# A transformer layer on one core: output tiles finished in pairs, weight splits ahead of finishing steps, and a later threshold search

## The reference, cut to what matters

```python
mix = einsum('bte,ed->btd', concatenate([att_out, hg_out]), w_out)   # 2048 x 1024 x 1024
x   = x + rms_norm(mix, norm_post_mix)
h2  = rms_norm(x, norm_pre_ffn)
ff  = silu(h2 @ w_gate) * (h2 @ w_up)                                 # 1024 -> 2816
ff  = ff @ w_down                                                     # 2816 -> 1024
x   = x + rms_norm(ff, norm_post_ffn)
```

## Time and profile before

| | us |
|---|---|
| median of the three runs | 3438.05 |
| lowest and highest of the three | 3437.49, 3439.71 |
| the profiled execution, its own time | 3442.69 |
| the span of its profile | 3440.9 |
| TensorE matmul busy | 3241.5 (94%) |
| VectorE busy | 2249.4 (65%) |
| ScalarE busy | 1500.5 (44%) |
| mean granted TensorE clock | 0.972 |

### The profile page before, as it was taken

The page is one execution under the profiler, slowest core; times in us unless marked ns, Lnnn a source line. Parts: engine busy times, 40 slices in busy tenths (PEclk is TensorE's granted clock), DMA queues, the critical chain, the costliest instruction groups (busy, mean ns, idle before and its releaser), DMA issues. The chain is left out here.

```text
span 3440.9 us, 46671 instructions
## 1 busy us (share of the span) xinstructions
PE 3241.5 (94%) x18176; PEld 2861.3 (83%) x18176; DVE 2249.4 (65%) x3721; ACT 1500.5 (44%) x2477; POOL 241.9 (7%) x400
## 2 busy tenths in 40 slices
PE   8999999999788799999979999997999999979998
PEld 8999999999666688888768888876988888868886
DVE  3466776888565676666777777778776765464445
ACT  3444545455354444343445444445454444333222
POOL 0000010000110100010110001011000000010000
PEclk9999999999899899999989999998999999989999
DMA  5434343434221322222422222134121111242233
GB/s 181 157 118 151 115 144 117 138 119 129 102 77 56 120 73 85 74 85 74 159 97 67 73 74 76 65 112 145 58 68 62 65 59 62 92 171 98 92 101 107
DMA packets 147501, 345.75 MB, mean 100 GB/s; under 512 B 15056, under 2 KB 35920, under 8 KB 145232
## 3 DMA queue, kind: packets, MB, share of 16 engines
q1 hardware_dynamic: 144976, 338.55, 29.4%
q10 hardware_dynamic: 2304, 4.20, 0.3%
HBM read 283.38 MB, written 59.31 MB: 100 GB/s over the span
## 5 line engine op out<-in xcount | busy, mean ns | idle before, releaser
L2018 PE MATMUL PJ_d<-h_hi,wd_hi 128*128 128x512 f32 (+1 forms) x1472 | 575.3, 391 | 13.8 <-DVE h_lo L1783 12.1
L2020 PE MATMUL PJ_d<-h_hi,wd_lo 128*128 128x512 f32 (+1 forms) x1472 | 563.5, 383 | 0.0
L2019 PE MATMUL PJ_d<-h_lo,wd_hi 128*128 128x512 f32 (+1 forms) x1472 | 562.4, 382 | 0.0
L1534 ACT ACTIVATE wd_hi<-wd_raw 128x512 fp32r<-128x512 f32 x568 | 345.7, 628 | 253.6 <-DMA wd_raw<-in_w_gu 160.8
L713 PE MATMUL PJ<-w_hi,h_hi 128*128 128x342 f32 (+1 forms) x1280 | 416.3, 325 | 5.9 <-DVE w_lo L539 5.9
L1778 DVE TENSOR_TENSOR wd_lo<-wd_raw,wd_hi 128x512 fp32r<-128x512 f32 x568 | 381.9, 690 | 47.0 <-ACT wd_hi L1534 44.2
L1529 ACT ACTIVATE pT<-SA 128x512 f32<-128x512 f32 (+3 forms) x320 | 156.5, 531 | 584.8 <-PE SA L1964 584.7
L714 PE MATMUL PJ<-w_lo,h_hi 128*128 128x342 f32 (+1 forms) x1280 | 409.4, 320 | 0.0
L715 PE MATMUL PJ<-w_hi,h_lo 128*128 128x342 f32 (+1 forms) x1280 | 409.3, 320 | 0.0
L1763 DVE CUSTOM_DVE_ANT_0 prob<-SA,bias 128x1024 f32<-128x1024 f32 (+7 forms) x192 | 170.1, 912 | 323.9 <-PE SA L1938 323.3
L2018 PEld LDWEIGHTS PJ_d<-h_hi,wd_hi 128*128 128x128 f32 x1472 | 279.5, 190 | 63.8 <-issue 11.8
(11 more groups left out here) (202 smaller groups left out, 5776.5 us busy)
## 6 DMA issues: line engine op xcount, KB each, us to landing
wd_raw<-in_w_gu SPq DMA_DIRECT2D x352, 256.0 KB, 3.0
wd_raw<-in_w_down SPq DMA_DIRECT2D x176, 256.0 KB, 2.6
w_raw<-in_w_in SPq DMA_DIRECT2D x40, 684.0 KB, 4.6
w_raw<-in_w_in SPq DMA_DIRECT2D x40, 676.0 KB, 4.5
row_h<-proj_d SPq DMA_DIRECT2D x16, 1024.0 KB, 6.7
proj_d<-stage SPq DMA_DIRECT2D x40, 342.0 KB, 4.5
proj_d<-stage SPq DMA_DIRECT2D x40, 338.0 KB, 5.0
x_d<-acc SPq DMA_DIRECT2D x24, 512.0 KB, 2.6
```

The source lines that it names most:

```text
L1534: s_.activation(w_hi[:, u % RING, :], w_raw[:, u % RING, :], ACT.Copy).then_inc(w_hi_ready, 1)
L2018: t.matmul(to[:, tok], w_hi[:, r, w], h_hi[:, c, tok], start=(c == 0 and part != 1), stop=False)
L2019: t.matmul(to[:, tok], w_hi[:, r, w], h_lo[:, c, tok], start=False, stop=False)
L2020: last = t.matmul(to[:, tok], w_lo[:, r, w], h_hi[:, c, tok], start=False, stop=(c == KD - 1 and part != 0))
```

## The change

The out items of a superblock run in pairs of tiles: both halves of tiles 0 and 1, then both of tiles 2 and 3. The turns of tiles 2 and 3 stand between the out items. Before, all four turns of s = 0 stood ahead of its outs, those of tiles 2 and 3 of s = 1 and 2 and of tile 2 of s = 3 among the last down items, and that of tile 3 of s = 3 behind the third out item. All turns and outs of s = 0 lie beside block 4, before and after. The transposes of the normalised tiles 0 and 1 come right after the last out item (gaps 0 and 1), and those of tiles 2 and 3 between the first halves of up 0. In VectorE's step the weight splits stand in front of `finish`. In blocks 4, 8 and 12 the threshold search begins at head 3 instead of head 0 and ends at the same place. SyncE's loads follow: the gains of s = 0 are loaded before its first turn, and for later superblocks norm_post_mix waits for all four finished tiles at the fourth out item; x of tiles 2 and 3 of s = 0 is loaded after turns 0 and 1, before after turn 3.

```diff
+    SEARCH = {(0, "A"): (0,), (0, "B"): (1,), (1, "A"): (2,), (2, "A"): (3,), (2, "B"): (4,), (3, "A"): (5,), (4, "A"): (6,),
+              (4, "B"): (7,), (5, "A"): (8,), (6, "A"): (9,), (6, "B"): (10,), (7, "A"): (11,)}
+    LATE_SEARCH = {(3, "A"): (0,), (3, "B"): (1,), (4, "A"): (2,), (4, "B"): (3, 4), (5, "A"): (5,), (5, "B"): (6, 7),
+                   (6, "A"): (8, 9), (6, "B"): (10,), (7, "A"): (11,)}
+    def search(b, h, name):
+        return (LATE_SEARCH if b and b % TS == 0 else SEARCH).get((h, name), ())
...
-    items += [("turn", 0, i) for i in range(TS)]
+    OUTS = [(n, i) for pair_of in range(0, TS, 2) for n in range(2) for i in (pair_of, pair_of + 1)]
     for s in range(NS):
-        outs = [("out", s, kg, n, i) for kg in range(1) for n in range(2) for i in range(TS)]
-        items += outs if s + 1 < NS else outs[:3] + [("turn", s, 3)] + outs[3:]
+        outs = [("out", s, 0, n, i) for n, i in OUTS]
+        if s == 0:
+            FIRST = len(items)
+            items += [("turn", 0, 0), ("turn", 0, 1)] + outs[:4] + [("turn", 0, 2), outs[4], ("turn", 0, 3)] + outs[5:]
+        elif s < LAST:
+            items += [outs[0], ("turn", s, 2), outs[1], ("turn", s, 3)] + outs[2:]
+        else:
+            items += [outs[0], ("turn", s, 2)] + outs[1:5] + [("turn", s, 3)] + outs[5:]
         first = [("up", s, 0, m, half, part) for part in range(2) for m in range(2) for half in range(2)]
-        items += [("gap", s, 0), ("gap", s, 1), ("gap", s, 2), ("gap", s, 3), first[0], ("gap", s, 4), first[1], first[2],
-                  ("gap", s, 5)] + first[3:]
+        items += [("gap", s, 0), ("gap", s, 1)] + first[:3] + [("gap", s, 2), first[3], ("gap", s, 3)] + first[4:]
...
-                if x == ("part", EARLY[-1], 1, 1, 2):
+                if x == ("part", EARLY[-1], 1, 1, 0):
                     load_mix(0, 0)
                     load_mix(0, 1)
+                    load_gain("norm_post_mix", g_mix_in)
+                    load_gain_ffn()
...
+                if x[0] == "out" and s and x[3:] in OUTS[:TS]:
+                    i = OUTS.index(x[3:])
+                    if i == TS - 1:
+                        sp.wait_ge(out_ready, TS * s)
                         load_gain("norm_post_mix", g_mix_in)
                         load_gain_ffn()
-                if x[0] == "out" and s and x[2:4] == (0, 0):
-                    i = x[4]
                     store_out(s - 1, i)
...
                 if last_out(n - 3):
                     add_mix(item_at(n - 3)[1], item_at(n - 3)[4])
+                for u in splits_at.get(n - 1, []):
+                    split_unit(u)
                 if last_down(n - 4):
                     finish(item_at(n - 4)[1], item_at(n - 4)[4])
-                for u in splits_at.get(n - 1, []):
-                    split_unit(u)
...
                     fill(("A", b, h))
-                    g = h // 2
-                    topk_part(b + 1, 3 * g if h % 2 == 0 else 3 * g + 2)
+                    for k in search(b, h, "A"):
+                        topk_part(b + 1, k)
                     fill(("B", b, h))
-                    if h % 2 == 0:
-                        topk_part(b + 1, 3 * g + 1)
+                    for k in search(b, h, "B"):
+                        topk_part(b + 1, k)
```

More of the change, by code:

```diff
@@ L861, in mixer_phase @@
                     items.append(("down", s, g, n, i))
-                    if g == NG - 1 and n == 0 and s + 1 < NS and i < (2 if s + 2 < NS else 1):
-                        items.append(("turn", s + 1, 2 + i))
     at = {x: n for n, x in enumerate(items)}
@@ L964, in mixer_phase @@
             window = window[PARTS_FROM:]
-            last = PARTS - 1
+            last = FIRST - 1
         mine = [x[0] for x in items[done:last + 1]]
@@ L1104, in enter_items @@
                     enter(key, "h")
-                if x[0] == "gap" and x[2] >= 2:
-                    h_order["hT", x[1], x[2] - 2] = len(h_order)
-                    enter(("hT", x[1], x[2] - 2), "h")
+                if x[0] == "gap":
+                    h_order["hT", x[1], x[2]] = len(h_order)
+                    enter(("hT", x[1], x[2]), "h")
         def enter_slot(key):
@@ L1589, in step @@
                     turned_high(("mT", x[1], x[2]), x[2], 0, KD // 2)
-                if x[0] == "gap" and x[2] >= 2:
-                    if x[2] == 2:
+                if x[0] == "gap":
+                    if x[2] == 0:
                         wait_summed(act, x[1], TS - 1)
-                    turned_high(("hT", x[1], x[2] - 2), x[2] - 2, 0, KD)
+                    turned_high(("hT", x[1], x[2]), x[2], 0, KD)
                 for u in splits_at.get(n, []):
@@ L1623, in _ @@
                         fill(("C", b, h))
-                    if h % 2 == 0:
-                        count(b + 1, 3 * (h // 2) + 1)
+                    for k in search(b, h, "B"):
+                        count(b + 1, k)
                 if b + 1 < NB:
@@ L1868, in step @@
                     norm_x1(item_at(n - 5)[1], item_at(n - 5)[4])
[L1869 to L1870 removed]
+                if x[0] == "gap":
+                    turned_low(("hT", x[1], x[2]), x[2], 0, KD)
                 if last_out(n - 3):
                     add_mix(item_at(n - 3)[1], item_at(n - 3)[4])
+                for u in splits_at.get(n - 1, []):
+                    split_unit(u)
                 if last_down(n - 4):
                     finish(item_at(n - 4)[1], item_at(n - 4)[4])
[L1875 to L1876 removed]
             def fill(key):
@@ L1996, in item @@
                     turn(("mT", s, x[2]), tile[:, mix_home(x[2]), :], KD // 2)
-                if x[0] == "gap" and x[2] >= 2:
-                    pe.wait_ge(xn_ready, TS * s + x[2] - 1)
-                    turn(("hT", s, x[2] - 2), tile[:, X_HOME[x[2] - 2], :], KD)
+                if x[0] == "gap":
+                    pe.wait_ge(xn_ready, TS * s + x[2] + 1)
+                    turn(("hT", s, x[2]), tile[:, X_HOME[x[2]], :], KD)
                 if x not in done_count:
```

16 lines of the change are left out of this document (7 added, 9 removed).

## The result

| | before | after |
|---|---|---|
| median of the runs, us | 3438.88 (3437.49 to 3440.76, four) | 3418.10 (3415.04 to 3419.83, four) |
| profiled execution, span | 3442.69, 3440.9 | 3419.83, 3418.0 |
| TensorE busy, rest of the span | 3241.5, 199.4 | 3248.8, 169.2 |
| mean granted clock | 0.972 | 0.976 |

The ratio is 0.9935 [0.9922, 0.9947]. The changed kernel is faster, by 43% of what the forecast had. The second phase's lines that the prediction names stand 13 higher than before: the bias of a score is L1776 (before L1763), a weight's low part L1791 (L1778), a tile's low part L1796 (L1783), add_mix L1840 and L1848, norm_x1 L1855 (L1842), the out copies L1571 (L1558), the tiles' transposes L1998 (L1985).

The account below looks back on a forecast made before the run. TensorE was taken to bound the kernel, with VectorE binding the handovers. Gains of 59.7 us less 4 (x) and 7.5 (clock) gave 48: 3394.5 profiled, 3390 as median of the runs, range 3366 to 3420.

Parts of the forecast that it names:

- 19.5: Tail: the gain forecast there in us, 8 from turn 2's load wait and 11.5 from the second window.
- x and norm_post_mix: Block 4 and tail: later loads make VectorE wait, 4 us taken for x and about 4 for norm_post_mix.
- the handovers stay VectorE-bound, only less: Superblock handovers: VectorE still bounds; 17 of 27.8 us stay in block 12, 18 of 31.5 in block 8, 15 of 20.4 in block 4.
- the late search as a gain: Heads 0 to 2: the search leaves VectorE there, 13.0 us in block 12, about 10 in block 8, about 7 in block 4.
- Rival A: Heads 3 to 6 of blocks 4, 8, 12: moved search parts become TensorE waits, 30 us plus 12 of clock; slower, 3450; 6%.
- the loss measure: TensorE's windows around handovers: idle time plus busy time times (1 - clock), 141.7 us in sum, taken as what can be won.
- the clock at 7.5: Handover stretches: 7.5 us taken off the gains for slower clock between short waits; 24 at worst, nothing at best.
- rival C: Handover stretches: many short waits keep the clock at 0.87 throughout, costing 24 us instead of 7.5; 3406; 12%.
- both waits go: Block 8: ScalarE's waits for an unstored earlier tile, 5.15 us, and for a weight unit, 4.10, vanish; part of 13.5.
- finish covers nobody's wait: VectorE's step: weight splits moved before finish cost nothing, coming 2.45 us earlier for TensorE.
- The 8 us for the tail's turn: Tail: turn 2 no longer stands 6.10 us for its load; 8 of 9.7 us go, clock's part included.
- B: Handovers: VectorE's total is the bound, so the pairs' gain moves into heads 5 to 7; 3409; 12%.

Follow-up runs that it names:

- e12: The changed kernel measured and profiled once more, nothing altered: 3417.73 us, ratio 0.9931 to the kernel before.
- e4: Changed kernel without VectorE's own halvings and the last adjusting loop of the search for blocks 5, 9 and 13 (other keys taken): 3408.04 us, ratio 0.9897.
- e1: Changed kernel with the threshold search of blocks 4, 8 and 12 back at heads 0 to 7: 3413.86 us, ratio 0.9920.
- e10: e1 with the edits of e7 and e9 together: 3416.53 us, ratio 0.9927.
- e13: e10 with the late search again (the edit of e1 taken back): 3421.88 us, ratio 0.9951.
- e2: Kernel before with nothing but the late search: 3440.42 us, ratio 0.9999.
- e6: e1 with the tiles of superblocks 0 and 1 not stored, so ScalarE waits only for the finished sum: 3406.43 us, ratio 0.9903.
- e7: e1 with finish three steps back instead of four, so sums go out an item earlier: 3411.36 us, ratio 0.9913.
- e9: e1 with turns 2 and 3 of superblocks 1 and 2 ahead of their outs: 3411.37 us, ratio 0.9912.
- e3: Changed kernel with the weight splits behind finish again: 3424.61 us, ratio 0.9953.
- e8: Kernel before with only turn 2 of the last superblock moved behind its first out item: 3440.01 us, ratio 0.9996.

## Why the prediction was right in sign and too large

**What held.** The pairs hide the finishing of tiles 0 and 1: L1842's 45.0 us became 6.3, "under 15". The tail's turn finds its load. ScalarE's wait for a weight unit in block 8 and TensorE's 5.00 behind it are gone; the longest wait for pT is 1.4. The tail gave 16.2 (13.6 in e12) of 19.5. x and norm_post_mix, for which 4 and 4 us were priced, delay little: VectorE stands 1.14 and 0.72 us for x in block 4, and in the tail not at all: there the gain is issued at 3014.86 and add_mix begins at 3019.86 behind the low part in front of it. In e12 it stands 0.83 for the gain and 1.71 for x in the tail as well. And the range held the time.

**The step that failed first: "the handovers stay VectorE-bound, only less".** From this came both the rest of 17, 18 and 15 us and the gain of the late search. VectorE's busy time from head 0 to 7 of block 12 was 84.6 us of 110.1, and in the stretch that the prediction names it was 57.9 of 67.6, 86% and not over nine tenths. e4 takes 39 us of it away and gets 10 to 13. What bounds the stretches in its place is not shown by a run. The waits that are left point at the chain that each tile goes through, of transposes, ScalarE's high part, VectorE's low part and the bank pair between them, beside the attention heads' own chain; busy us of one engine don't price that.

**The second: the late search as a gain.** It was counted into the 5.4, 13.5 and 10.8. It costs 4.2 us with the change (e1), 5.3 beside e10's order (e13), and is neutral alone (e2). Where it frees VectorE, in heads 0 to 2, that saved 3.25 us of waits, in block 8; where it goes, scores are read later and the transposes behind them wait, 2.96 us there. Rival A had the place and the sign, but charged all 30 moved us as waits; 4 to 5 us of time is what they are.

**The third, and the largest: the loss measure.** Summed over the eight windows it fell from 141.7 to 90.7, by 51, where the forecast had 48. So by its own measure the forecast came true (block 12's second window went to 12.62 + 0.09 x 67.38 = 18.7, where 17 was forecast), and yet the span fell by 22.9. Split the measure in two. Its idle part fell from 97.0 to 62.2, by 34.8, and the idle time of the whole span by 30.2: that part is sound. Its clock part, (1 - clock) x busy, fell from 44.7 to 28.5 and promised 16.2 us, while the busy time rose by 7.3. These 23.5 and the 4.6 of the idle part are the 28 that are missing. Where the 23.5 went can be counted, by laying the trace's records of the half clock over TensorE's busy spans. First, the clock of a window is a mean over its time, and the half clock lies over idle time more than its share: before, over 52.2 of the 97.0 idle us of the eight windows and over 70.7 of their 283.0 busy us. Over idle time it costs nothing; take that time away and the mean rises though no matmul runs faster. The busy time at half clock in these windows fell from 70.7 to 58.9, worth 5.9 us and not 16.2. Second, outside the windows it rose, by 22.8 (the whole span: 115.3 before, 126.3 after), which costs 11.4; the windows did not hold the same work, and block 12's heads hold 568 matmuls and not 560, since its turns 2 and 3 went into them. The last 1.8 us of the 7.3 are no half clock. In e12 the same stretches have 57.3 and the whole span 116.2, so that outside them it rose by 14.3, which costs 7.1.

**The fourth: the clock at 7.5.** The term stood for what the clock would still cost in the second windows of the four handovers. By the records they hold 45.6 us of busy time at half clock, 44.1 in e12, after 47.5 before: that costs 22.8 and 22.0 us, and it cost 23.8 before. So next to nothing of it went, and rival C's 24 had the size. Counted over wider stretches, from head 0 to the next block's head 0, in blocks 8 and 12 with the 45 us ahead of head 0, and over 115 us of the tail from head 7 of block 15:

| | idle: before, after, e12 | busy at half clock: before, after, e12 |
|---|---|---|
| block 4 | 20.0, 15.1, 15.1 | 17.6, 29.7, 29.7 |
| block 8 | 26.8, 25.2, 24.9 | 22.0, 13.4, 13.7 |
| block 12 | 26.9, 17.6, 18.8 | 14.9, 25.9, 13.7 |
| tail | 28.6, 14.5, 15.9 | 16.2, 10.8, 12.9 |

Over the four, the busy time at half clock went from 70.7 to 79.8 in the one execution, which costs half of 9.1, and to 70.0 in the other. What repeats is block 4: it rose by 12.1, and the half of it, 6, is more than the 4.9 that idle time gave. So the first handover gained nothing. In the tail and in block 8 the clock improved. The Trainium skill, TensorE: Matmul & The Clock Gate, section A second HAM failure mode: psum-queue depth-cycling, has the rule that short idle times between groups keep the clock swinging. Block 4 agrees with it (ten waits of 0.7 to 2.2 us in the place of nine of up to 6.6, clock 0.80 after 0.81). In the tail the waits became shorter too, eight of up to 4.4 us in the place of nine of up to 9.2, and the clock rose from 0.83 to 0.93; what makes the difference no run shows.

**The fifth: "both waits go".** Of ScalarE's two only w_gu's went. The first two tiles' sums of the superblock before are still finished four steps back, beside the first outs, and their copies wait for the stores; the turns' high parts stand behind them now. It is worth 7 us at most (e6, with the transfers gone too). e7 shortens it by moving the finish, and e9 does away with it by moving the turns; each gives some 2.5.

**The sixth and seventh, small and opposite.** The splits in front, costed at nothing, are worth 6 us (e3): the cover that the prediction named, "finish covers nobody's wait", was true of finish, but behind it a weight's low part was what TensorE waited for, in block 8, block 12 and the tail. The 8 us for the tail's turn were not there alone (e8); that the tail came out near its 19.5, at 16.2 or 13.6, is in part luck: the splits, costed at nothing, shorten its longest such wait from 6.2 to 3.6.

In sum: 48 forecast, 20.8 measured. By kind, what is missing is clock, 23.5 of 28 in the two profiles, and 10.3 of these were never there, but came of the mean clock. By cause, the runs show 4 to 5 for the late search, as idle time and clock in a mix that they don't settle, and 2.5 to 7 for the wait behind the stores; the two ways of counting overlap. B's 3409 was nearest in number, but its mechanism, VectorE's total, is what e4 excludes in block 12 and leaves at most half of elsewhere.

**What stays open.** Why e7 and e9 don't add is not known. What part of e4's rest is chain and what is clock was not separated. e7 and e9, at 3411.4, are the fastest that still compute everything: 0.9913 and 0.9912, below the changed kernel's interval at their medians though the intervals overlap; e1's one line gives most of it.

## What to carry to other kernels

Ask of a handover not how busy its engines are but what chain each tile must pass, and take an engine's work away once to see whether its sum binds: 39 us less work gave 10 to 13 here. Price idle time and busy time at half clock separately, record by record, and by stretches that hold the same work. When long waits become short ones, look at TensorE's busy time for the same matmuls, in two profiles of the same kernel: what it grows by is given back, and it was 7.3 us in one and 3.3 in the other.

## What the runs showed that was not expected

The granted clock in one place differs between executions of the same program: in block 12 the half clock covered 25.9 us of busy time in one and 13.7 in the other, with idle times within 1.2 us of each other, and the stretch was 3.6 us longer. Moving VectorE's work within eight heads changed TensorE's idle time by 0.6 us and its busy time by 6.7 (e1), of which such a difference between executions can be a part; the medians of e1 against after and of e10 against e13 show that 4 to 5 us of time hold.
